# Mixture of experts on one core: routing by tile pairs inside the out-projection, rows scattered to expert slots

## The reference

```
cond = silu(c);  sh1, sc1, g1, sh2, sc2, g2 = split(cond @ ada_w + ada_b, 6)
hn = rmsnorm(x, norm1_g) * (1 + sc1) + sh1
u = hn @ w_in                                   # 1024 -> 2 x 1024
a, b from the gates of the convolved half;  hs = linear scan over time
x = x + g1 * ((hs * gelu(gate)) @ w_out)
hn = rmsnorm(x, norm2_g) * (1 + sc2) + sh2
probs = softmax(hn @ router_w + router_b)       # 16 experts, 4 groups of 4
best  = argmax over groups of the sum of the group's two largest probs
the two largest probs of that group, divided by their sum, are the gates
out = sum over the two chosen experts of gate_e * (silu(hn @ w_gate[e]) * (hn @ w_up[e])) @ w_down[e]
x = x + g2 * out
return rmsnorm(x, final_norm_g)
```

## Time and profile before

| | us |
|---|---|
| median of three runs (lowest, highest) | 1336.77 (1336.19, 1342.6) |
| the profiled execution | 1335.74 |
| its span in the trace | 1334.2 |
| TensorE busy | 1082.2 (81%) |
| VectorE busy | 769.5 (58%) |
| ScalarE busy | 567.3 (43%) |
| GpSimd busy | 563.5 (42%) |

### The profile page before, as it was taken

How to read it: one execution, slowest core, us unless ns; L and a number is a source line. 1 busy time by engine, 2 the same in 40 slices (tenths; PEclk the granted TensorE clock), 3 DMA queues, 4 the chain that set the end, 5 groups by cost and what they waited for, 6 DMA issues and landing times. The chain is left out here.

```text
span 1334.2 us, 19676 instructions
## 1 busy us (share of the span) xinstructions
PE 1082.2 (81%) x4894; PEld 866.6 (65%) x4895; DVE 769.5 (58%) x874; ACT 567.3 (43%) x792; POOL 563.5 (42%) x394
## 2 busy tenths in 40 slices
PE   1459999999999994899999814899999999989300
PEld 0247778778778773688888714677777776767200
DVE  6984676667667664545343376354544545445288
ACT  1554666766776673422222220333433334334033
POOL 0686625525526420145455243333433333334273
PEclk9999999999999997899999855999999999999755
DMA  8544314313313201833324144466756567667498
GB/s 303 175 89 151 99 33 130 84 46 114 93 53 114 63 16 38 311 126 98 139 94 141 48 142 174 135 210 209 262 199 228 189 211 241 206 207 236 145 350 324
DMA packets 126572, 207.59 MB, mean 156 GB/s; under 512 B 16961, under 2 KB 84545, under 8 KB 126417
## 3 DMA queue, kind: packets, MB, share of 16 engines
q1 hardware_dynamic: 106096, 132.81, 30.7%
q0 software_dynamic: 14832, 54.01, 12.0%
q10 hardware_dynamic: 5616, 20.45, 3.8%
HBM read 156.36 MB, written 50.87 MB: 155 GB/s over the span
## 5 line engine op out<-in xcount | busy, mean ns | idle before, releaser
L1214 POOL TENSOR_TENSOR w_lo<-w_raw,w_hi 128x1536 f32 x30 | 107.1, 3570 | 157.8 <-ACT w_hi L1272 157.8
L1377 PE MATMUL e_gu<-w_hi,e_xh 128*128 x312 | 130.2, 417 | 13.7 <-issue 5.0
L1272 ACT ACTIVATE w_hi<-w_raw 128x1536 f32 x60 | 88.3, 1486 | 121.1 <-PE e_pd L1402 46.3
L849 PE MATMUL po<-wo_hi,b_yh 128*128 128x512 f32 x256 | 102.9, 402 | 25.6 <-DVE wo_lo L779 25.6
L1379 PE MATMUL e_gu<-w_hi,e_xl 128*128 x312 | 123.5, 396 | 0.0
L1378 PE MATMUL e_gu<-w_lo,e_xh 128*128 x312 | 122.8, 394 | 0.0
L823 POOL TENSOR_TENSOR x<-x,b_xr 128x1024 f32 (+1 forms) x15 | 49.1, 3273 | 171.9 <-DVE x L787 171.9
L531 DVE SCALAR_TENSOR_TENSOR XB<-xu,conv_w,XB 128x512 f32<-128x512 f32 x96 | 92.6, 965 | 42.2 <-ACT XB L401 38.5
L624 PE MATMUL px<-hT_hi,wx_hi 128*128 128x512 f32 x256 | 101.7, 397 | 5.1 <-DVE wx_lo L465 5.1
L624 PE MATMUL pg<-hT_hi,wg_hi 128*128 128x512 f32 x256 | 104.2, 407 | 0.0
L625 PE MATMUL px<-hT_lo,wx_hi 128*128 128x512 f32 x256 | 101.6, 397 | 0.0
(11 more groups left out here) (260 smaller groups left out, 2639.4 us busy)
## 6 DMA issues: line engine op xcount, KB each, us to landing
yslot_scratch<-e_y ACTq DMA_DIRECT2D x39, 512.0 KB
stg<-in_ada_w_dram POOLq DMA_DIRECT2D x32, 512.0 KB, 4.2
w_raw<-in_moe_w_gate_dram SPq DMA_DIRECT2D x32, 384.0 KB, 3.3
w_raw<-in_moe_w_up_dram SPq DMA_DIRECT2D x32, 384.0 KB, 4.0
n_ada<-in_ada_w_dram SPq DMA_DIRECT2D x16, 512.0 KB, 4.8
n_x<-in_x_dram SPq DMA_DIRECT2D x16, 512.0 KB, 3.4
y_scratch<-M SPq DMA_DIRECT2D x16, 512.0 KB, 3.0
b_yt<-y_scratch SPq DMA_DIRECT2D x16, 512.0 KB, 5.3
```

The costliest lines, as they stand in the source:

```text
L849: nc.tensor.matmul(po[u][:, cols], yh[u][:, tok], wo_hi[:, k, cols], start=(k == 0), stop=False)
L1214: tensor_tensor(w["lo"][:, ds(off + q * QW, QW)], w["raw"][:, q % 2], w["hi"][:, ds(off + q * QW, QW)].bitcast(F32), ALU.subtract).then_in ...
L1272: nc.scalar.activation(w["hi"][:, ds(off + q * QW, QW)], w["raw"][:, q % 2], ACT.Copy).then_inc(w["hi_done"], 1)
L1377: nc.tensor.matmul(gu[:], xh[:, tok], hi, start=(k == 0), stop=False)
```

## The change

The stages dispatch and combine go. Their work is done elsewhere:

- Each expert owns a fixed region of 2048 slots in DRAM. There are three such arrays: records of four words (rec_scratch), normed rows (hn2_slots), residual rows (x2_slots). During the recurrence SP copies 128 rows of x to the start of each of the 16 regions of both row arrays (32 DRAM-to-DRAM copies of 0.5 MB), so that unused slots hold numbers. One 0.5 MB store fills the records.
- **out_and_route** replaces out_and_norm and the routing of dispatch. Transposes and router products work on the residual tile one step after its matmuls; norm scale, shift and bias enter through router_wm and constant logits. The addition of x moves from GpSimd to VectorE. The reciprocal root is made on GpSimd in five one-column instructions. For each pair of tiles VectorE chooses (31 dependent instructions) in the odd step and assigns slots (15) in the even one. GpSimd then issues five scatters per tile: two of records, two of the normed rows to both experts' slots, one of the residual row to the slot of the earlier expert. x2 is a ring of eight tiles.
- The tables are made after the last tile, beside the first expert's weights. Experts are visited in the order 0, 4, 8, 12, 1, 5, ..., so that a token's two experts are at least four blocks apart.
- In **experts** ScalarE's queue loads a block's rows and residual rows plainly. The gate is applied in the activation product. VectorE scales by g2row, adds the residual rows and, one block later, norms; ScalarE squares; GpSimd makes the root and issues two scatters with a bounds check: the sum goes to the token's second slot, the normed row to the output. A record holds an address beyond the bound for the one that doesn't apply, so each row is written by one of the two.

```diff
@@ lru, sync
+            def fill_pads(j):
+                for i in range(E // KD):
+                    for t in slots:
+                        sp.dma_start(t[ds(j * (E // KD * S) + i * S, P), :], io["x"][0, 0:P, :]).then_inc(pad_filled, 16)
@@ body: before store_y(j, 0)
+                fill_pads(j)
@@ out_and_route, vector (new)
+            def gate(it):
+                dve.wait_ge(mm, it + 1)
+                v.tensor_tensor(gy[:], po[it % 2][:], g1row[:], ALU.mult).then_inc(gated, 1)
+                dve.wait_ge(gated, it + 1)
+                v.tensor_tensor(x2[:, it % RING], gy[:], x2[:, it % RING], ALU.add).then_inc(resid, 1)
...
+            dve.wait_ge(rows_in, 16 * 4)
+            for s in range(1, NT + 1):
+                gate(s - 1)
+                if s >= 2:
+                    logits(s - 2)
+                if s >= 3 and s % 2 == 1:
+                    softmax_in((s - 3) // 2)
+                if s + 1 < NT:
+                    low(s + 1)
+                if s >= 3 and s % 2 == 1:
+                    choose((s - 3) // 2)
+                if s >= 4 and s % 2 == 0:
+                    assign((s - 4) // 2)
+                if s < NT:
+                    scale(s - 1)
@@ out_and_route, gpsimd (new)
+            def send(it):
+                r = it % RING
+                pool.wait_ge(placed, it // GT + 1)
+                for c in range(TOPK):
+                    pool.indirect_dma_start(dr["rec"], rows(pos[:, c, it:it + 1]), rec[:, c, it], None).then_inc(sent[r], 16)
+                pool.wait_ge(shifted, it + 1)
+                for c in range(TOPK):
+                    pool.indirect_dma_start(dr["h"], rows(pos[:, c, it:it + 1]), hn[:, r], None).then_inc(sent[r], 16)
+                pool.indirect_dma_start(dr["x2"], rows(first_pos[:, it:it + 1]), x2[:, r], None).then_inc(sent[r], 16)
@@ out_and_route, tensor (new)
+            for s in range(1, NT):
+                pe.wait_ge(ylo, s + 1)
+                main(s, 0, range(KD))
+                if s >= 4 and s % 2 == 0:
+                    rank((s - 4) // 2)
+                turn(s - 1)
+                main(s, 1, range(KD // 2))
+                route(s - 1)
+                main(s, 1, range(KD // 2, KD)).then_inc(mm, 1)
@@ experts, gpsimd
-                gather(i + LEAD)
+            with pool.Fori(3, nless) as i:
+                scatter_out(i - 2)      # waits out_done (i-2) * 16, out_ready i - 1
+                scatter_acc(i - 1)      # waits acc_out (i-1) * 16, acc_ready i
                 low_w(pool, nc.gpsimd.tensor_tensor, i + 1, 1)
+                root(i - 1)             # waits squared i; five instructions on one column
@@ experts, scalar
+            with act.Fori(4, nless) as i:
+                square(i - 1)           # waits acc_ready i
+                load_x(i)               # waits xa_in i * 16, acc_ready i, acc_out (i-3) * 16
                 high_a(i + 1)
                 tanh(i + 2)
-                store(i)
                 high_x(i + 3)           # first load_h(i + 4)
                 high_w(i + 2)
@@ experts, vector
                 low_a(i + 1)
                 act_product(i + 2)
                 low_x(i + 3)
+                normed(i - 1)           # waits rstd_ready i, out_done (i-1) * 16
+                accumulate(i)           # waits xa_in (i+1) * 16, squared i, out_ready i, acc_out i * 16
                 y_scaled(i + 1)         # now waits acc_ready i + 1, before y_out
                 low_w(dve, nc.vector.tensor_tensor, i + 2, 0, dues)
@@ build
-        combine(nc, sem, cst, io, tab, x2, yslot_dram, out)
```

More of the change, by code:

```diff
@@ L940, in dispatch @@
-        ends_ready, filled = sem("ends_ready"), sem("yslot_filled")
-        gate2 = gates[:].rearrange("p c t -> p (c t)")
+        wo_hi, wo_lo, yh, yl = w["wo_hi"], w["wo_lo"], w["yh"], w["yl"]
+        ring = sb("b_ring", [P, RING, D])
+        wr = hn = ring
+        x2 = sb("x2", [P, RING, D])
+        g1row, sh2, gy, hT = w["g1row"], w["sh2"], w["gy"], w["hT"]
+        gain, sc2 = hT, sb("sc2", [P, D])
+        yt = sb("b_yt", [P, 2, D])
+        ssq, var, root0, part, rstd = [sb(n, [P, 2]) for n in ("b_ssq", "b_var", "b_root0", "b_part", "b_rstd")]
@@ new lines, in _ @@
+            load_y(0)
+            for k in range(KD):
+                sp.dma_start(wr[:, k], w_v[k]).then_inc(wr_in[k // 2], 16)
+            load_x(0)
+            load_y(1)
+            sp.dma_start(g1row[:], dr["mod"][0, 0:D].partition_broadcast(P)).then_inc(g1_in, 16)
+            with nc.allow_non_contiguous_dma(reason="small vectors by channel"):
+                for i, src in enumerate((dr["mod"][0, D:2 * D], dr["mod"][0, 2 * D:3 * D], io["norm2_g"][0])):
+                    sp.dma_start(cols[:, i], src.rearrange("(k p) -> p k", p=P), allow_slow_non_contiguous=True)\
+                        .then_inc(cols_in, 16)
@@ new lines, in exponent, with high_w @@
+            def exponent(g):
+                act.wait_ge(exp_in, g + 1)
+                nc.scalar.activation(prob[:], work[:], ACT.Exp).then_inc(exp_out, 1)
+            def high_w(q):
+                wcols = slice(q * QW, (q + 1) * QW)
+                act.wait_ge(w["in"][q], 16 * QLOADS[q])
+                nc.scalar.activation(w["hi"][:, wcols], w["raw"][:, q % 2], ACT.Copy).then_inc(w["hi_done"], 1)
+            high(0)
+            for k in range(KD):
+                act.wait_ge(wr_in[k // 2], 32)
+                nc.scalar.activation(wo_hi[:, k], wr[:, k], ACT.Copy).then_inc(wo_h, 1)
@@ L1009, in _ @@
+            high(1)
+            for s in range(1, NT + 1):
+                if s + 1 < NT:
+                    high(s + 1)
+                squares(s - 1)
+                if s >= 3 and s % 2 == 1:
+                    exponent((s - 3) // 2)
+                evacuate(s - 1)
+            act.wait_ge(mm, NT)
+            high_w(0)
+            exponent(NT // 2 - 1)
+            for q in range(1, NQ):
+                high_w(q)
         @block.vector
@@ new lines, in _ @@
+            g = NT // 2 - 1
+            logits(NT - 1)
+            softmax_in(g)
+            scale(NT - 1)
+            choose(g)
+            assign(g)
+            for q in range(2):
+                dve.wait_ge(w["hi_done"], q + 1)
+                wcols = slice(q * QW, (q + 1) * QW)
+                v.tensor_tensor(w["lo"][:, wcols], w["raw"][:, q % 2], w["hi"][:, wcols].bitcast(F32),
+                                ALU.subtract).then_inc(w["lo_done"][q % 2], 1)
+            done(v.scalar_tensor_tensor(limit[:], base[:], -float(P), origin[:], ALU.add, ALU.max))
@@ L1168, in experts @@
+            rank(NT // 2 - 2)
+            turn(NT - 1)
+            route(NT - 1)
+            rank(NT // 2 - 1)
+def experts(nc, sem, cst, io, tab, w, dr, g2row, out):
     ctx = ExitStack()
@@ L1198, in _ @@
                 load_quarter(sp, io, w, 1, q)
-            with sp.Fori(2, E) as e:
+            for b in range(E, MAXB):
+                load_rec(b)
+            for e in range(2, E):
                 for q in range(NQ):
@@ new lines, in build @@
+        for n in ("hi", "lo"):
+            at = -(-nc.sbuf_base // 32) * 32
+            w[n] = sb("w_" + n, [P, 2 * WE], F32R)
+            over = lambda name, shape, start, d=F32R: nc.alloc_sbuf_tensor_at(name, shape, d, offset=at + 4 * start)
+            w["wo_" + n] = over("wo_" + n, [P, KD, D], 0)
+            w["y" + n[0]] = [over(f"b_y{n[0]}{u}", [P, D], (KD + u) * D) for u in range(2)]
+            for i, name in enumerate(("gy", "hT") if n == "hi" else ("g1row", "sh2")):
+                w[name] = over("b_" + name, [P, D], (KD + 2 + i) * D, F32)
```

995 lines of the change are left out of this document (519 added, 476 removed).

## The result

The changed kernel takes 1387.38 us (median of four runs, 1385.26 to 1391.37) where the kernel before takes 1336.48 beside it (1334.11 to 1342.6): ratio 1.038, 95% interval [1.033, 1.042]. It is 51 us slower; 1285 was predicted. The span of its profiled execution is 1387.8 us.

The account below looks back on a forecast made before the run. TensorE was taken to bound recurrence, out-projection and experts, but not routing and combine (154 us). Span 1334.2 - 20 (routing) + 35 (experts) - 66 (end) = 1283 us, forecast as 1285 us measured, range 1240 to 1345.

Parts of the forecast that it names:

- start of the out-projection: Before the first gating product: VectorE waits for four broadcast rows and three vectors, +4 us (0 to +8).
- fifteen steps: Out-projection from first to last gating product: 13.9 us a tile instead of 13.17, +11 us (+7 to +40).
- last projection to first expert product: Leftover routing on GpSimd and VectorE, then the experts' start: 52 us instead of 87, -35 (-42 to -20).
- end: After the last scaling in the experts: 16 us left instead of 81.6, -66 us (-69 to -58).
- the ring of root, norm, scatters and remainder: Experts: GpSimd and VectorE work from one block's root to the next, mean 8.9 to 10.9 us beside TensorE's 9.86.
- rival 3: Experts: GpSimd's root and scatters bound the block, mean 14 us, +145, kernel slower at 1395 us; chance 0.13.
- The sum of 9.9 to 11.4 us: Experts: root, norm, two scatters, index copy, tests and weight remainder added up for a block with a remainder.
- the 5.5 to 7 of blocks without a remainder: Experts: the same GpSimd and VectorE cycle in us for blocks in which GpSimd subtracts no weights.
- Two limits of nearly one size: Experts: GpSimd's cycle and TensorE, with opposite patterns, together cost 0.9 us a block, +35 us (0 to +100).
- The second ring: Experts: accumulation waits until the previous sum has landed, 8.5 to 10.3 us a block, taken as inside the first.
- Rival 2: Out-projection: VectorE and GpSimd block each other, 15.5 to 16 us a tile, +30, 1315 us; chance 0.15.
- Rival 4: Experts: scatter writes cannot be taken beside weight loads, weights come late, the end's gain returns as waits, about 1335; chance 0.04.

Follow-up runs that it names:

- the extra load: Changed kernel with ScalarE's queue loading each block's 128 normed rows a second time into a buffer nothing reads: 1391.0 us.
- the best version: Changed kernel with remainders on VectorE, four raw weight buffers, two sum and output buffers, shared record loads, earlier out-projection start and one-word table: 1280.8 us, 0.961 of kernel before.
- the remainder edit: Changed kernel with GpSimd splitting no weights in the experts; VectorE subtracts the low parts of the odd quarters too: 1342.8 us.

## Why the prediction was wrong

| step | predicted us | measured us |
|---|---|---|
| recurrence | 0 (0 to +6) | 0; +3.4 from the unchanged first norm |
| start of the out-projection | +4 (0 to +8) | +10.7 |
| fifteen steps | +11 (+7 to +40) | +8.6 |
| last projection to first expert product | -35 (-42 to -20) | -24.2 |
| first expert product to first scaling | none | +2.7 |
| experts, first to last scaling | +35 (0 to +100) | +111.4 |
| end | -66 (-69 to -58) | -58.9 |
| sum | -51 | +53.7 |

- **Experts: the step that failed.** The mechanism was there, the ring of root, norm, scatters and remainder with its place and its order; rival 3 named the result almost to the number (1395, "slower from 12.6 us a block") but by prices that did not come: the root is 2.15 us and not 4.5, the scatters 0.97 and 1.47 us and not 1.81, so that its nearness is luck. The sum of 9.9 to 11.4 us (its terms as listed add up to 10.1 to 11.5) against 13.2 to 14.2 measured is short by two terms. The tests, put at 0.8, take 1.4 (2.41 less 0.97) or 2.5 us; no row stood behind that number. One word for them gave 32 us, VectorE's and ScalarE's reads included. And from the root's end to the scatter's start it is 2.45 us, where the norm alone (1.35) was counted: the scatter starts 0.85 us and more after its last wait, as the earlier trace rows already showed (the 0.77 before the gather).
- **The mean.** I averaged 9.9 to 11.4 with the 5.5 to 7 of blocks without a remainder. But those take 9.0 to 9.5 us: from 1202.45 to 1211.35 GpSimd needs 8.9 us from root to root without a remainder. And nothing is caught up (with one buffer for the sum, the output and the root, which is my reading): 27 of 38 distances carry the long ring in full, and one more is the stall of 29.0. "Two limits of nearly one size" was right and priced at 0.9 where it was 2.9 a block, 0.35 of this from the records (13 us in 38 blocks).
- **The second ring** was called inside the first. It is in the changed kernel, with a landing of 5.8 us in the median; with GpSimd relieved it stood in the chain with landings of 7.7 to 9.1, and a second buffer for it gave 8 us.
- **Records.** Not in the prediction at all. 48 small loads were a part of the change whose issues I did not count: 1.06 to 1.13 us each on SP, of which the issuing instruction is 0.34 and the rest the read of the row number.
- **Start.** The lateness of the rows was foreseen, but not its size: they let VectorE go at 565.15 us, not around 558, and the wait for them stood ahead of the first gating product, which with the wait behind it waits only for TensorE (0.53 us). The vectors were priced by their landing (3.1 us) and not by what their issue holds up, which was about 2 us. The Trainium skill (DMA: Bandwidth & Descriptors, Rules for kernel authors) has one descriptor per element for such vectors. The issue of 1024 elements took 8.75 us for one, 2.86 for two others and 0.89 on GpSimd's queue, so the count of elements alone does not give it; what else holds SP at this place was not tried.
- **Fifteen steps.** 13.75 us a tile, 13.9 predicted. Rival 2 did not come: VectorE's low subtraction takes 1224 ns in the median, where the earlier trace rows has 3336.
- **To the first expert product.** Right in kind. Five tiles of scatters, not four, were left after the last gating product, and their last instruction ended at 814.2; GpSimd's remainder behind them then held VectorE's table once:

```profile
814.19 3.43 POOL L1143 TENSOR_TENSOR w_lo<-w_raw,w_hi 128x1536 fp32r<-128x1536 f32 x1
...
813.60 4.09 DVE L1054 TENSOR_TENSOR t_split<-d_second,d_flag 128x48 int32<-128x48 f32 x1
```

- **End.** 22.7 us, 16 predicted. Two things were not in the list. The last accumulation starts at 1370.7, 5.5 us after the last scaling: it stands in VectorE's program behind the norm of the block before, which waits for GpSimd's scatter and root.

```profile
1369.20 1.28 DVE L1523 SCALAR_TENSOR_TENSOR e_ob<-e_ab,e_rstd,e_fg 128x1024 f32<-128x1024 f32 x1 [4.03 <-POOL e_rstd L1324]
1370.68 1.23 DVE L1514 TENSOR_TENSOR e_ab<-e_y,e_xa 128x1024 f32<-128x1024 f32 x1 [0.20 <-DVE e_ob L1523]
1377.74 1.10 POOL L1304 DMA_INDIRECT out_dram<-e_ob,e_idx_o  x1 [2.14 <-DVE e_ob L1523]
```

And from the end of the last scatter's instruction, at 1378.84, to the end of the span it is 9.0 us, where a landing of 5.3 to 7.1 and 1 us for the end were counted.
- **Rival 4** and every reading by transfers fall with the extra load (+1.4 us of scalings, within the spread, for 0.5 MB a block more) and with the best version, which keeps the scatters.

Shown by an experiment: remainder, reads, records, the wait at the start (by the trace of its edit), and that traffic, copies, weight buffers, root and index copy are not it in the changed kernel. Tried one by one on the changed kernel the gains are 42, 36 and 13 us of scalings for remainder, reads and records. The first two overlap, since the remainder edit also takes GpSimd's reads away. Together with the buffers of weights, sums and outputs they give 105.6 of the 111.4 us. Left open: the share of each buffer once the reads are short, and the 22 us block (a sole block of an expert, where both halves are split at once: 17.4 in the best version; my reading, not tested).

## What to carry to other kernels

An engine that is half idle by its busy share can still be the bound: add up its whole program for the worst kind of block, reads of registers and branches included, then follow the ring through every other engine that it waits for; shortening one engine's part gives only what it takes from that ring. Count the issues of small loads and what stands behind them in the queue, and put a wait where its data is first used. Pack the values that a block's control flow reads into one word: here it was worth 32 us alone and 33 in the best version.

## What the runs showed of the hardware

- A read of a table value from SBUF into a register takes 0.29 us in the median on GpSimd and 0.30 on VectorE in the changed kernel, and up to 0.69 in the lines shown, with 0.15 to 0.19 of register work behind each; four of them on GpSimd were more than VectorE's norm of 1.28 us could hide.
- GpSimd's copy of one column takes 0.18 us alone and 1.24 when it starts 0.09 us behind VectorE's norm, which lasts 1.28 and has two inputs in SBUF; it ends when the norm does (1077.67 and 1077.62). The Trainium skill (SBUF — State Buffer, Who interferes with whom) has the two exclude each other for a whole instruction; the trace agrees. Moving the copy away gained nothing here.
- The power function on one column takes 0.58 us on GpSimd, the other steps of the root 0.19 to 0.27; a scatter with a bounds check (rows whose address lies beyond the bound are left out) takes 0.98 us in the median for the sum and 1.47 for the output.
- Early in a stage that issues some 20 loads in a row, single issues on SP took 8.75 us (a vector of 4 KB by channel), 8.91 (router_b, in the kernel before) and 3.77 (a row of 512 KB), where most others of 512 KB took 0.4 to 0.5. The same vector took 0.89 on GpSimd's queue.
